# Gathering the tokens of a mixture of experts: 256 slots at a time from two float32r parts, all within the first expert's block

## The reference

```
def hierarchical_moe(hn, w_rg, w_re, w1, w3, w2):
    xf = hn.reshape(n, d_)
    p_group = softmax(xf @ w_rg);  g_idx = argmax(p_group)        # 4 groups
    fine = (xf @ w_re) of the group chosen                       # 8 experts in each
    top_v, top_i = lax.top_k(fine, 2)
    gate = g_gate * softmax(top_v)
    ...                                                           # slots sorted by expert
    def expert_block(args):
        xblk, e = args
        return (silu(xblk @ w1[e]) * (xblk @ w3[e])) @ w2[e]
    ...
    y = zeros.at[slot_tok].add(yb * slot_w)
```

## Time and profile before

| | us |
|---|---|
| median of the three runs shown (1946.41 to 1949.05) | 1948.79 |
| the profiled execution, whole | 1946.12 |
| its span, from the first to the last instruction | 1944.3 |
| PE busy | 1818.2 |
| DVE busy | 819.8 |
| ACT busy | 523.2 |

### The profile page before, as it was taken

How to read it: one execution, slowest core, us unless ns; L and a number is a source line. 1 busy time by engine, 2 the same in 40 slices (tenths; PEclk the granted TensorE clock), 3 DMA queues, 4 the chain that set the end, 5 groups by cost and what they waited for, 6 DMA issues and landing times.

```text
span 1944.3 us, 25101 instructions
## 1 busy us (share of the span) xinstructions
PE 1818.2 (94%) x10194; PEld 1174.3 (60%) x10194; DVE 819.8 (42%) x1178; ACT 523.2 (27%) x764; POOL 59.7 (3%) x56
## 2 busy tenths in 40 slices
PE   6999899999989899999889998989989989899996
PEld 6989799899767789988754433323323333333332
DVE  3544554688554555434443332232232222232233
ACT  4444344644343444434420010000010000010012
POOL 0000000132211000000000000000000000000000
PEclk9999899999999999999989999999999999899999
DMA  7545455444455456426659999999999999999995
GB/s 267 193 152 174 130 174 165 129 152 138 129 123 141 173 194 189 152 87 224 274 223 380 397 427 428 429 428 421 428 429 428 428 429 429 428 428 428 428 429 250
DMA packets 107127, 556.77 MB, mean 286 GB/s; under 512 B 12352, under 2 KB 12584, under 8 KB 81192
## 3 DMA queue, kind: packets, MB, share of 16 engines
q1 hardware_dynamic: 97672, 431.90, 57.4%
q10 hardware_dynamic: 8352, 121.64, 14.9%
q0 software_dynamic: 1024, 2.10, 1.6%
HBM read 553.51 MB, written 2.10 MB: 286 GB/s over the span
## 4 chain that ended last, share of the span: by engine, by line
PE 75%; DMA 19%; DVE 4%; ACT 1%; issue 1%; SPq 0%; ACTq 0%; DVEq 0%
DMA arena<-in_moe_w_dram 18%; PE ps L922 17%; PE ps L950 6%; PE ps L587 6%; PE ps L581 6%; PE ps L582 6%; PE ps L583 6%; PE ps L589 6%; PE ps L588 6%; PE ps L933 3%; PE ps L967 2%; PE ps L879 2%; PE ps L728 1%; PE ps L549 1%; DVE w_lo L1502 1%
## 5 line engine op out<-in xcount | busy, mean ns | idle before, releaser
L922 PE MATMUL ps<-arena 128*64 128x512 f32 x2048 | 497.6, 620 | 54.7 <-DMA arena<-in_moe_w_dram 53.0
L1502 DVE TENSOR_TENSOR w_lo<-arena,w_hi 128x1024 fp32r<-128x1024 f32 x264 | 317.1, 1244 | 287.4 <-ACT w_hi L1086 287.0
L1086 ACT ACTIVATE w_hi<-arena 128x1024 fp32r<-128x1024 f32 x264 | 264.7, 1052 | 325.2 <-PE ps L583 178.7
L922 PEld LDWEIGHTS ps<-arena 128*64 128x64 f32 x2048 | 136.1, 139 | 314.2 <-issue 248.6
L2067 DVE TENSOR_TENSOR arena<-ps,arena 128x1024 f32<-128x1024 f32 x128 | 156.6, 1225 | 239.9 <-PE ps L967 239.9
L950 PE MATMUL ps<-arena 128*64 128x512 f32 x1024 | 227.3, 596 | 2.6 <-DVE arena L2044 1.8
L950 PEld LDWEIGHTS ps<-arena 128*64 128x64 f32 x1024 | 73.3, 138 | 148.7 <-issue 144.0
L581 PE MATMUL ps<-x_hi,w_hi 128*128 128x256 f32 x512 | 146.3, 286 | 3.2 <-DVE w_lo L1502 3.2
L583 PE MATMUL ps<-x_hi,w_lo 128*128 128x256 f32 x512 | 145.6, 284 | 0.0
L582 PE MATMUL ps<-x_lo,w_hi 128*128 128x256 f32 x512 | 145.6, 284 | 0.0
L2061 DVE TENSOR_TENSOR d_lo<-ps,d_hi 128x512 fp32r<-128x512 f32 x64 | 41.2, 686 | 233.4 <-ACT d_hi L1373 233.4
(11 more groups left out here) (365 smaller groups left out, 2608.2 us busy)
## 6 DMA issues: line engine op xcount, KB each, us to landing
arena<-in_moe_w_dram SPq DMA_DIRECT2D x133, 2048.0 KB, 19.1
arena<-in_moe_w_dram ACTq DMA_DIRECT2D x58, 2048.0 KB, 14.3
arena<-in_w_in_dram SPq DMA_DIRECT2D x52, 1024.0 KB, 5.0
arena<-in_xa_wk_dram SPq DMA_DIRECT2D x16, 1024.0 KB, 5.1
arena<-in_xa_wv_dram SPq DMA_DIRECT2D x16, 1024.0 KB, 5.1
arena<-in_w_out_dram SPq DMA_DIRECT2D x16, 1024.0 KB, 5.0
arena<-in_xa_wq_dram SPq DMA_DIRECT2D x16, 1024.0 KB, 5.0
arena<-in_xa_wo_dram SPq DMA_DIRECT2D x16, 1024.0 KB, 5.1
```

What stands on the lines that cost most here:

```text
L922: last = mm(ps[rows_, m, :], xe[par][:, ECH * i + c, :], ring_up[m][i][:, c, :], start=(i == 0 and c < 2), stop=(i == ECH - 1 and c >= 2))
L1086: fn(hi_ring[(2 * n + u) % 4][:], ring_a[i][:, 2 * u:2 * u + 2, :], ACT.Copy).then_inc(S["w_hi"], 1)
L1502: V.tensor_tensor(w_lo[i][:, 2 * u:2 * u + 2, :], ring_a[i][:, 2 * u:2 * u + 2, :], hi_ring[(2 * n + u) % 4][:].bitcast(F32), ALU.subtract ...
```

## The change

All 512 slots are now gathered within block 0, 256 at a time. The float32 product is replaced by two products of float32r operands, a narrower form of float32: ACT writes `hx_hi`, the part that float32r holds, and DVE writes `hx_lo`, what is left (`low_tokens`, four passes of 1024 elements for each partition); `sel` is float32r as well. The first 256 slots are gathered in two parts, `first_gather(0)` before the first chunk and `first_gather(2)` behind the second chunk of block 0, high parts first, low parts behind a wait for `hx_dve`. The last 256 slots come in four quarters, `gather_quarter(b)`, each behind one chunk of the second up matrix. All four use the banks 6 and 7, so quarter b waits until `gathered(b - 1)` has emptied them (`g_dve` 4 + b). The four `gathered` passes stand on DVE behind the tokens of expert 1 and the memsets. The gathers in blocks 1 to 4 are gone.

```diff
-        hx, fgain = arena(64, NT, D), arena(64, D)
+        fgain = arena(64, D)
+        hx_hi, hx_lo = at_r("hx_hi", 64, [P, NT, KT, P]), at_r("hx_lo", 16, [P, KT, SLOTS + EB])
...
-        sel, sel_g, sel_t = arena(80, NT, SLOTS), arena(52, NT, SLOTS), arena(56, SLOTS)
+        sel, sel_g, sel_t = at_r("sel", 80, [P, NT, SLOTS]), arena(52, NT, SLOTS), arena(56, SLOTS)
+        HALF = SLOTS // 2
+        tokens_lo = lambda j: slice(HALF + j * P, HALF + (j + 1) * P)
...
-            sp.wait_ge(S["g_pe"], 10)
+            sp.wait_ge(S["g_pe"], 8)
...
-            def gather(t, b, at):
-
-                for c in range(4):
-                    for j in range(NT):
-                        last = mm(ps[:, at, c * P:(c + 1) * P], hx[:, j, (4 * b + c) * P:(4 * b + c + 1) * P], sel[:, j, t * P:(t + 1) * P],
-                                  start=(j == 0), stop=(j == NT - 1))
+            def gather(half, k, at, lo):
+
+                for j in range(NT):
+                    part = hx_lo[:, k, tokens_lo(j)] if lo else hx_hi[:, j, k, :]
+                    last = mm(at, part, sel[:, j, HALF * half:HALF * (half + 1)], start=(not lo and j == 0 and k % 2 == 0), stop=(lo and j == NT - 1),
+                              skip_group_check=True)
                 return last
+            def first_gather(b0):
+
+                at = lambda k: ps[:, 4 + k % 8 // 2, HALF * (k % 2):HALF * (k % 2 + 1)]
+                for k in range(4 * b0, 4 * b0 + 8):
+                    gather(0, k, at(k), False)
+                for b in range(b0, b0 + 2):
+                    pe.wait_ge(S["hx_dve"], 2 if b < 2 else 4)
+                    for k in range(4 * b, 4 * b + 4):
+                        last = gather(0, k, at(k), True)
+                    last.then_inc(S["g_pe"], 1)
...
-            for b in range(4):
-                gather(0, b, 4 + b).then_inc(S["g_pe"], 1)
-
-            def gather_half(t, half):
-
-                if t == 1 and half == 0:
+            first_gather(0)
+
+            def gather_quarter(b):
+
+                if b == 0:
                     pe.wait_ge(S["sel_dve"], 2)
-                pe.wait_ge(S["g_dve"], 2 * t + half + 2)
-                for b in range(2):
-                    last = gather(t, 2 * half + b, 6 + b)
+                pe.wait_ge(S["g_dve"], 4 + b)
+                for lo in (False, True):
+                    for k in range(4 * b, 4 * b + 4):
+                        last = gather(1, k, ps[:, 6 + k % 4 // 2, HALF * (k % 2):HALF * (k % 2 + 1)], lo)
                 last.then_inc(S["g_pe"], 1)
...
                 up(n, 0, 1, par)
-                if halves:
-                    if back >= 1:
-                        pe.wait_ge(S["c_add"], 4 * back)
-                    gather_half(*halves[0])
+                if back is None and isinstance(n, int) and n == 0:
+                    pe.wait_ge(S["g_act"], 2)
+                    first_gather(2)
...
-                for half in halves[1:]:
-                    gather_half(*half)
                 up(n, 0, 2, par)
                 up(n, 0, 3, par)
                 for i in range(ECH):
                     up(n, 1, i, par)
-                    if halves and i == 0:
-                        pe.wait_ge(S["g_dve"], 2 * halves[-1][0] + halves[-1][1] + 3)
+                    if back is None and isinstance(n, int) and n == 0:
+                        if i == 0:
+                            pe.wait_ge(S["g_act"], 4)
+                        gather_quarter(i)
+                    if isinstance(n, int) and n == 1 and i == 0:
+                        pe.wait_ge(S["g_dve"], 8)
...
-            block_n(1, 0, 1, ((1, 0), (1, 1)))
-            block_n(2, 1, 0, ((2, 0), (2, 1)))
-            block_n(3, 2, 1, ((3, 0),))
-            block_n(4, 3, 0, ((3, 1),))
+            block_n(1, 0, 1)
+            block_n(2, 1, 0)
+            block_n(3, 2, 1)
+            block_n(4, 3, 0)
...
-                fn(hx[:, j, :].rearrange("p (k q) -> p k q", k=KT), h[:, j, :].rearrange("p (q k) -> p k q", k=KT), ACT.Copy,
+                fn(hx_hi[:, j], h[:, j, :].rearrange("p (q k) -> p k q", k=KT), ACT.Copy,
                    scale=st[:, 40 + j:41 + j]).then_inc(S["hx_act"], 1)
...
-                    last = fn(xsT[:, k, 0:P], ps[:, 4 + b, c * P:(c + 1) * P], ACT.Copy, scale=ffn_gain[:, k:k + 1])
+                    last = fn(xsT[:, k, 0:HALF], ps[:, 4 + k % 8 // 2, HALF * (k % 2):HALF * (k % 2 + 1)], ACT.Copy, scale=ffn_gain[:, k:k + 1])
...
+            def low_tokens(j, half):
+
+                ks = slice(8 * half, 8 * half + 8)
+                dve.wait_ge(S["hx_act"], j + 1)
+                V.scalar_tensor_tensor(hx_lo[:, ks, tokens_lo(j)], h[:, j, :].rearrange("p (q k) -> p k q", k=KT)[:, ks, :],
+                                       st[:, 40 + j:41 + j], hx_hi[:, j, ks, :].bitcast(F32), ALU.mult, ALU.subtract).then_inc(S["hx_dve"], 1)
+
+            low_tokens(0, 0)
             dve.wait_ge(S["r_pe"], 2)
...
-            def gathered(t, half):
-                dve.wait_ge(S["g_pe"], 2 * t + half + 3)
-                for b in range(2):
-                    k = 8 * half + 4 * b
-                    last = V.tensor_tensor(xsT[:, k:k + 4, t * P:(t + 1) * P], bank(6 + b, 4, P), bc_last(ffn_gain[:, k:k + 4], P), ALU.mult)
-                last.then_inc(S["g_dve"], 1)
+            def gathered(b):
+                dve.wait_ge(S["g_pe"], 5 + b)
+                got = ps[:, 6:8, :].rearrange("p a (c t) -> p (a c) t", t=HALF)
+                V.tensor_tensor(xsT[:, 4 * b:4 * b + 4, HALF:SLOTS], got, bc_last(ffn_gain[:, 4 * b:4 * b + 4], HALF), ALU.mult).then_inc(S["g_dve"], 1)
...
-            select(0, P)
+            select(0, HALF)
+            low_tokens(1, 0)
             V.scalar_tensor_tensor(negm, gmax8[:, :, 0], -1.0, st[:, 40:42], ALU.mult, ALU.mult).then_inc(S["r_dve"], 1)
             step(V.tensor_tensor(vdif, fmax8[:, :, 1], fmax8[:, :, 0], ALU.subtract))
             V.tensor_tensor(vdif, vdif, st[:, 40:42], ALU.mult).then_inc(S["r_dve"], 1)
             dve.wait_ge(S["ffn_in"], 16)
             first_tokens(0)
-            select(P, SLOTS)
             first_tokens(1)
+            low_tokens(0, 1)
+            low_tokens(1, 1)
...
             step(weighted(0))
             first_tokens(3)
             weighted(1).then_inc(S["selg_dve"], 1)
+            select(HALF, SLOTS)
...
             V.memset(wrow[:, SLOTS:], 0.0)
             V.memset(xsT[:, :, SLOTS:], 0.0)
+            for b in range(4):
+                gathered(b)
             dve.wait_ge(S["r_pe"], 3)
...
-            block_n(0, 0, 0, True, ((1, 0), (1, 1)))
-            block_n(1, start_of(1), 1, True, ((2, 0), (2, 1)))
+            block_n(0, 0, 0, True)
+            block_n(1, start_of(1), 1, True)
             dve.wait_ge(S["g_dve"], 8)
-            block_n(2, start_of(2), 0, True, ((3, 0),))
-            block_n(3, start_of(3), 1, True, ((3, 1),))
-            dve.wait_ge(S["g_dve"], 10)
+            block_n(2, start_of(2), 0, True)
+            block_n(3, start_of(3), 1, True)
             block_n(4, start_of(4), 0, True)
```

More of the change, by code:

```diff
@@ L308, in program @@
                   "xs_pe", "xs_max", "xs_p", "xs_diag", "xs_t", "xs_tev", "xs_o", "xs_oa", "xs_od",
-                  "sq_part", "rms_dve", "hx_act", "sel_dve", "selg_dve",
+                  "sq_part", "rms_dve", "hx_act", "hx_dve", "sel_dve", "selg_dve",
                   "r_pe", "r_dve", "r_act", "g_pe", "g_act", "g_dve", "row_pe", "row_act", "tab_dve",
@@ L969, in comb, with block_n @@
                 last.then_inc(S["c_pe"], 1)
-            def block_n(n, back, par, halves=(), behind=False):
+            def block_n(n, back, par, behind=False):
                 if behind:
@@ L1965, in first_tokens @@
                 dve.wait_ge(S["g_pe"], b + 1)
-                V.tensor_tensor(xe[0][:, 4 * b:4 * b + 4, :], bank(4 + b, 4, P)[:, :, 0:EB], bc_last(ffn_gain[:, 4 * b:4 * b + 4], EB),
+                got = ps[:, 4 + 2 * (b % 2):6 + 2 * (b % 2), :].rearrange("p a (c t) -> p (a c) t", t=HALF)
+                V.tensor_tensor(xe[0][:, 4 * b:4 * b + 4, :], got[:, :, 0:EB], bc_last(ffn_gain[:, 4 * b:4 * b + 4], EB),
                                 ALU.mult).then_inc(S["g_dve"], 1)
-            def gathered(t, half):
-                dve.wait_ge(S["g_pe"], 2 * t + half + 3)
-                for b in range(2):
-                    k = 8 * half + 4 * b
-                    last = V.tensor_tensor(xsT[:, k:k + 4, t * P:(t + 1) * P], bank(6 + b, 4, P), bc_last(ffn_gain[:, k:k + 4], P), ALU.mult)
-                last.then_inc(S["g_dve"], 1)
+            def gathered(b):
+                dve.wait_ge(S["g_pe"], 5 + b)
+                got = ps[:, 6:8, :].rearrange("p a (c t) -> p (a c) t", t=HALF)
+                V.tensor_tensor(xsT[:, 4 * b:4 * b + 4, HALF:SLOTS], got, bc_last(ffn_gain[:, 4 * b:4 * b + 4], HALF), ALU.mult).then_inc(S["g_dve"], 1)
             def weighted(j):
@@ L2067, in add, with block_n @@
```

(11 more changed lines are left out.)

## The result

The changed kernel takes 1953.24 us (median of 18 runs, 1951.24 to 1955.67), the kernel before 1948.66 us (18 runs, 1946.13 to 1953.99). The ratio is 1.0023 with a 95% interval of 1.0016 to 1.0029: 4.6 us slower (by the interval 3.1 to 5.7 us), small, but the interval excludes no change. The forecast was 1954.8 us, slower. The profiled execution of the changed kernel took 1951.24 us with a span of 1949.4 us; before the span was 1944.3 us, so the two profiles differ by 5.1 us.

What follows compares the result with a forecast made beforehand. DMA weight transfers bound the long loop, PE from 988 to 1132 us; 2.7 MB fewer by 1132.5 us is 6.3 us, taken as +6.0 us on the median 1948.79 us: 1954.8 us, range 1948.0 to 1960.5 us.

Steps and rivals of the forecast that it cites:

- Up to the stall: Block 0: gather starts at 976.9 us, two chunks end at 987.0 us, the low_tokens passes cost nothing.
- The stall: Block 0: quarter 1 waits for gathered(0) to free its banks, PE idle 5.6 us until 1005.7 us.
- The sum over DVE's chain: DVE in block 0: passes added from 990.3 us put the start of gathered(0) at 1004.3 us.
- The clock: Behind the stall: granted clock falls to half, costing 2.1 us, lower end 0, upper end 6.1 us.
- the short stretch: Behind the stall: a half-clock stretch with PE busy for 4.2 us of it, costing 2.1 us.
- the rival of the long one: Behind the stall: clock at 0.50 for 10 us or more, block 1 at 1026 us, +10 us, 1959 us; chance 0.10.
- Block 1: Start of block 1: at 1022.1 us, 16.9 us later than 1005.25 us before.
- From block 1 to the end: Queue full from 1030.2 us on; 2.7 MB less moved by 1132.5 us, which is 6.3 us.
- The count by landings: Up to 1132.5 us: counting weight transfers landed instead of bytes gives about 4 to 5 us.
- PE's lead: Blocks 1 to 4: 23.6 us shorter on PE, block 5 starts at 1125.7 us, 7 us early, and waits for weights.
- A small stall: Block 0: DVE reaches gathered(0) sooner or the clock holds; half the stall gives +1.1 us, 1949.9 us; chance 0.20.
- The end follows PE: Blocks 1 to 5: releases set the pace, block 5's 7 us lead moves the end, 1942 us; 0.12 including other gains.

Runs made afterwards that it cites:

- two independent ways of removing this wait: The changed kernel with two gathered passes moved earlier on DVE, 1946.81 us; the changed kernel with quarter 1 in banks 4 and 5, 1948.36 us.
- the run that kept the clock: The changed kernel with 38 extra matmuls, results unread, filling PE's wait ahead of quarter 1: 1951.07 us.

## Why the prediction was right

**Up to the stall.** Gather from 976.9 us: exact. First two chunks done at 987.0 us: exact. The four `low_tokens` passes took 1.93 to 2.02 us, at the upper end of their forecast of 1.2 to 2.0 us, which came from the strided ACT row, and all were hidden, the first with 0.18 us to spare. The Trainium skill (page SBUF — State Buffer, section "Door 1: The DMA port swizzle") says that an access which crosses to a new 16-byte line pays a penalty. These passes agree in kind, against 1.2 us for the nearest pass of 1024 elements without that stride.

**The stall.** Forecast 5.6 us, until 1005.7 us; measured 4.84 us, until 1005.20 us. Both ends were off by little: quarter 0's last chunk ended at 1000.3 us and the memset at 1004.0 us. The sum over DVE's chain was the step that carried the sign, and two independent ways of removing this wait turned the loss into none. The shorter stall was in part made up by the gather itself: sixteen float32r matmuls took 2.1 us, where the forecast had 1.9 us.

**The clock.** Forecast 2.1 us of half clock; 2.0 us by the run that kept the clock. It is the short stretch, so the rival of the long one did not come about here. Which of the two would come rested on how often each was seen and on no cause, so that the short one came is in part luck. Longer ones did come, but behind waits for weights in block 4. The Trainium skill (page TensorE: Matmul & The Clock Gate, section "HAM oscillation — how this bites in real kernels") says that a wait for data inside a loop lets the array's clock fall. The rows at 0.50 agree, after waits of 4.84 and 3.29 us, and had the clock held through the stall, filling the wait would not have gained 2.2 us.

**Block 1** at 1022.1 us: measured 1021.74 us. Four transfers landed before the reload of block 1, as forecast; that the stall would open a gap ahead of the fourth was not in it, and by the count of bytes it makes no difference.

**From block 1 to the end.** The mechanism held, the size of one term did not: the difference in bytes was put at 2.7 MB and 6.3 us, measured 2.1 MB and 4.9 us. Most of the 0.6 MB is in the stretch from 1025 to 1051 us, 9.5 MB where a flow from 1030.2 us on makes 8.9 MB: the two parts of it are

```profile
1025.00:1030.20 5.20, 5.20 (x28) 2.10 (x29) 2.29 (x5) 0.13 (x1) 0.00 (x0) 1.00 0.34 104
1030.20:1051.00 20.80, 20.80 (x105) 7.46 (x102) 6.19 (x6) 2.50 (x5) 0.00 (x0) 1.00 1.00 429
```

The flow had begun about 1.3 us before 1030.2 us (104 x 5.2 is 0.54 MB, at 428 GB/s 1.3 us). The count by landings, 4 to 5 us, was the better of the two, and the +6.0 us that I took lay between; +4.6 us came. That PE's lead would go into waits for weights held, only earlier: in block 4, so that block 5 started at 1133.26 us and not at 1125.7 us.

**The other rivals.** A small stall: no, the chain was as long as its terms. The end follows PE: no, the lead of 7 us that it needed at block 5 was gone in block 4, in a wait for weights, and there a delay of 2.65 us changed the time by nothing that can be told. What the account left out is that this slack is small: it had the queue full from 1030.2 us on and asked no more, and the run with 40 matmuls in block 4 shows that a full queue can still be emptied.

## What to carry to other kernels

Where a stream of weights bounds the kernel behind some point, price an edit ahead of it by the bytes that are through the queue when it fills for good, not by the engine's busy time: a gather of half the matmul time cost 4.6 us here because all of it had moved ahead of block 1, where the queue stood empty, and had brought a wait of 4.84 us with it. Work that an engine does while the queue is full is nearly free up to the length of the transfers (29.9 us against 29.4 us here), so fill that first. When two consumers share a buffer, add up the chain ahead of the instruction that frees it on its own in-order engine; moving that instruction and the next of its kind was worth 6.4 us.

## What the runs showed that I had not expected

The full queue hides less than its share of 1.0 suggests: 2.65 us in block 4 cost at most about 1 us, 5.57 us cost 3.6 us. A wait for weights may make this worse by itself, since the clock that falls with it delays the next requests: waits of 3.29 and 4.06 us in block 4 (changed kernel, and the run with 40 matmuls there) came with 10.24 and 13.65 us at 0.50. No run kept the clock up there, so what this costs is not shown.

Where such stretches fall near the end moves single executions by some us. In the profile of the kernel with the quarters in blocks 1 and 2 (1946.0 us, against a median of 1941.9 us) one of them lies 100 us before the end:

```profile
1830.04:1843.69 13.65, 12.20 (x36) 5.74 (x38) 2.29 (x5) 0.38 (x1) 0.00 (x0) 0.50 1.01 429
```

The queue is full all through it, and no wait for weights is left from 1880 us on, where the changed kernel still has two of about 1 us: there PE, not the queue, came last: the chain that ended last has no transfer in it from 1850 us on. Why the stretch falls there in some executions stays open.
